# Two-block hybrid network, 256 tokens, float32 split products: LayerNorm row operations spread between halves of weights, the decay series moved to the first output products, the first head's convolution ahead of the gate scans

## What is computed

```python
for l in range(DEPTH):   # 2
    x = layer_norm(ALPHA * x + 0.5 * swiglu(x, ffn_w1[l, 0], ffn_w2[l, 0]), ln_g[l, 0], ln_b[l, 0])
    mix = hybrid_mixer(x, w_in[l], ...)
    x = layer_norm(ALPHA * x + mix, ln_g[l, 1], ln_b[l, 1])
    x = layer_norm(ALPHA * x + 0.5 * swiglu(x, ffn_w1[l, 1], ffn_w2[l, 1]), ln_g[l, 2], ln_b[l, 2])

# in the mixer's recurrence, per channel:
log_a = -LRU_C * gate_rec * jax.nn.softplus(-a_param)
a = jnp.exp(log_a)
mult = jnp.sqrt(-jnp.expm1(2.0 * log_a))

# in the last mixer, per head (8 heads):
qk = jax.nn.silu(dw_conv(jnp.concatenate([q, k], axis=-1), conv_w, conv_b))   # 3 taps along the tokens
state, hs = mlstm_chunkwise(q, k, v, i_pre, f_pre, state)                       # gates: cumulative sums and maxima
```

## Time and profile before

| | |
|---|---|
| median of 3 runs | 2186.13 us (2181.99 to 2194.47) |
| the profiled execution's own time | 2188.97 us |
| its span, first to last instruction | 2187.2 us |
| PE busy | 2145.6 us, 98% of the span |
| DVE busy | 1431.6 us, 65% |
| ACT busy | 900.1 us, 41% |
| mean granted TensorE clock | 0.994 of full speed |

### The profile page before, as it was taken

How to read it: one execution, slowest core, us unless ns; L and a number is a source line. 1 busy time by engine, 2 the same in 40 slices (tenths; PEclk the granted TensorE clock), 3 DMA queues, 4 the chain that set the end, 5 groups by cost and what they waited for, 6 DMA issues and landing times. The chain is left out here.

```text
span 2187.2 us, 35415 instructions
## 1 busy us (share of the span) xinstructions
PE 2145.6 (98%) x14986; PEld 1945.9 (89%) x14986; DVE 1431.6 (65%) x2084; ACT 900.1 (41%) x1060; POOL 18.1 (1%) x35
## 2 busy tenths in 40 slices
PE   9999999999999999999999999999999989999998
PEld 8998999999989989999899768888788878999996
DVE  5556877685566548876765677877666456666665
ACT  4333365343343334383433353222344334443442
POOL 0000000000000000000000000000000000000000
PEclk9999999999999999999999999999999999999999
DMA  9654555666566555455564432222112232232331
GB/s 346 228 181 186 193 193 200 233 259 232 183 257 235 193 193 191 179 180 203 217 240 185 159 129 77 77 77 77 65 52 78 87 116 78 97 136 78 116 116 58
DMA packets 28925, 348.94 MB, mean 160 GB/s; under 512 B 2976, under 2 KB 5408, under 8 KB 8352
## 3 DMA queue, kind: packets, MB, share of 16 engines
q1 hardware_dynamic: 24672, 313.42, 38.8%
q0 software_dynamic: 4096, 33.26, 3.8%
HBM read 345.62 MB, written 1.05 MB: 158 GB/s over the span
## 5 line engine op out<-in xcount | busy, mean ns | idle before, releaser
L2071 DVE TENSOR_TENSOR w_lo<-ring,w_hi 128x2048 fp32r<-128x2048 f32 x290 | 661.8, 2290 | 417.6 <-ACT w_hi L1497 413.0
L1497 ACT ACTIVATE w_hi<-ring 128x2048 fp32r<-128x2048 f32 x290 | 555.7, 1917 | 700.0 <-PE banks L778 472.3
L773 PE MATMUL banks<-x_hi,w_hi 128*128 128x256 f32 x2112 | 505.2, 280 | 0.2 <-ACT w_hi L1497 0.2
L774 PE MATMUL banks<-x_lo,w_hi 128*128 128x256 f32 x2112 | 504.2, 280 | 0.0
L773 PEld LDWEIGHTS banks<-x_hi,w_hi 128*128 128x128 f32 x2112 | 399.2, 189 | 1.1 <-issue 1.1
L774 PEld LDWEIGHTS banks<-x_lo,w_hi 128*128 128x128 f32 x2112 | 399.5, 189 | 0.0
L778 PE MATMUL banks<-x_hi,w_lo 128*128 128x256 f32 x2112 | 288.8, 279 | 7.9 <-DVE w_lo L2071 7.9
L778 PEld LDWEIGHTS banks<-x_hi,w_lo 128*128 128x128 f32 x2112 | 264.5, 189 | 8.7 <-DVE w_lo L2071 8.7
L1068 PE MATMUL banks<-x_hi,w_hi 128*128 128x512 f32 (+1 forms) x664 | 236.8, 370 | 1.2 <-DVE x_lo L2412 1.2
L1069 PE MATMUL banks<-x_lo,w_hi 128*128 128x512 f32 (+1 forms) x664 | 229.1, 358 | 0.0
L1531 ACT ACTIVATE arena<-banks 128x512 f32<-128x512 f32 (+5 forms) x178 | 79.7, 471 | 284.4 <-PE banks L1072 165.2
(11 more groups left out here) (367 smaller groups left out, 2808.4 us busy)
## 6 DMA issues: line engine op xcount, KB each, us to landing
ring<-weights SPq DMA_DIRECT2D x147, 2048.0 KB, 7.8
arena<-mods POOLq DMA_DIRECT2D x11, 2048.0 KB, 11.6
bcast<-lnrows POOLq DMA_DIRECT2D x12, 512.0 KB, 10.0
ring<-weights SPq DMA_DIRECT2D x2, 1024.0 KB, 9.9
xrow<-x SPq DMA_DIRECT2D x1, 1024.0 KB, 5.2
arena<-hy_consts POOLq DMA_DIRECT2D x1, 1024.0 KB, 15.4
xrow<-ctx_rows POOLq DMA_DIRECT2D x1, 1024.0 KB, 5.3
out<-xrow SPq DMA_DIRECT2D x4, 256.0 KB, 2.0
```

Source lines behind the costliest of these rows:

```text
L773: nc.tensor.matmul(out, hi[:, k, t * P:(t + 1) * P], x_h[:, k, :], start=k == 0, stop=False)
L774: nc.tensor.matmul(out, hi[:, k, t * P:(t + 1) * P], x_l[:, k, :], start=False, stop=False)
L1497: nc.scalar.activation(hi, raw, ACT.Copy).then_inc(w_hi_done, 1)
L2071: v.tensor_tensor(lo, raw, hi.bitcast(F32), ALU.subtract).then_inc(w_lo_done, 1)
```

## The change

It has three parts, and adds or removes no product and no transfer.

1. `rows_gained` becomes `row_gained(l, n, r, step)`, one operation of 128x1024 at a time. In the mixer the four stand behind the `weights_lo` calls of `yg` 3 0, 3 1, 4 0 and 4 1; in the feed-forwards behind those of j = 2 and j = 3, one per half.
2. The decay series is cut into four steps, which stand behind the first four `weights_lo` calls of the first feed-forward's output products (`down`), and ACT's Exp moves behind the first `weights_hi` there.
3. `qk_conv(0)`, the convolution of head 0, moves ahead of the gate scans, and its two tanh on ACT move ahead of the next `weights_hi`.

```diff
--- before.py
+++ after.py
@@ -1524,6 +1524,9 @@
                         mod_copy(MOD_GROUPS.index((l, "up", f)))
                 for q in range(DOWN_HALVES - 2):
                     after(l, "down", f, q // 2, q % 2)
+                    if (l, f, q) == (0, 0, 0):
+                        act.wait_ge(sp_abs, 1)
+                        nc.scalar.activation(small[:, 16:32], small[:, 0:16], ACT.Exp).then_inc(sp_exp, 1)
                     if (l, f) == (DEPTH - 1, 1):
...
             copy(cond[:].rearrange("p a b -> p (a b)"), c2[:, C2["cond"]:C2["cond"] + 16], S2["cond_done"], ACT.Silu)
-            act.wait_ge(sp_abs, 1)
-            nc.scalar.activation(small[:, 16:32], small[:, 0:16], ACT.Exp).then_inc(sp_exp, 1)
             for l in range(DEPTH):
                 half_b, half_m, decay = half_bs[:, l, :], half_ms[:, l, :], decays[:, l, :]
                 ffn(l, 0)
...
                     A.drain().then_inc(S2["gate_rows"], 1)
                     act.sem_inc(free[b], 1)
+                    ml_silu(0)
                 after(DEPTH, "qkv", i, 0)
...
                     act.wait_ge(S2["gate_ab"], 2)
                     copy(g_u[0:64, 0:SEQ], g_u[0:64, SEQ:ROWS], S2["em_in"], ACT.Exp, scale=-1.0)
-                    ml_silu(0)
                 b = filled(act, i, "ml", "z")
...
-            def rows_gained(l, n):
-
-                filled(dve, l, "layer", "turn", n, 3)
-                dve.wait_ge(row_in, 32 * (3 * l + n) + 32)
-                for r in range(RT):
-                    v.tensor_tensor(xrow[:, r, :], xrow[:, r, :], bcast[:, 0, :], ALU.mult)
-                v.drain()
-                for r in range(RT):
-                    x = v.tensor_tensor(xrow[:, r, :], xrow[:, r, :], bcast[:, 1, :], ALU.add)
-                x.then_inc(S2["rows_ok"], 1)
-                v.drain()
+            def row_gained(l, n, r, step):
+
+                if r + step == 0:
+                    filled(dve, l, "layer", "turn", n, 3)
+                    dve.wait_ge(row_in, 32 * (3 * l + n) + 32)
+                v.drain()
+                x = v.tensor_tensor(xrow[:, r, :], xrow[:, r, :], bcast[:, step, :], (ALU.mult, ALU.add)[step])
+                if r + step == 2:
+                    x.then_inc(S2["rows_ok"], 1)
+                    v.drain()
 
             def ffn(l, f):
                 for j in range(FJ):
-                    if j == 2 and l + f:
-                        rows_gained(*((l, 1) if f else (l - 1, 2)))
-                    after(l, "up", f, j, 0)
-                    after(l, "up", f, j, 1)
+                    for side in range(2):
+                        after(l, "up", f, j, side)
+                        if j in (2, 3) and l + f:
+                            row_gained(*((l, 1) if f else (l - 1, 2)), side, j - 2)
                     b = filled(dve, l, "layer", "up", f, j, 1)
                     released(dve, l, "layer", "up", f, j, 0)
...
                     after(l, "down", f, q // 2, q % 2)
+                    if l + f == 0 and q < 4:
+                        decay_series(q)
                     if q == FT // 4:
...
-            def log1p(dst, y, tmp, tmp2):
...
-                for odd in (13.0, 11.0, 9.0, 7.0, 5.0, 3.0, 1.0):
...
+            def decay_series(step):
+
+                dst, y, tmp, tmp2 = (small[:, 16 * n:16 * n + 16] for n in (3, 1, 4, 5))
+                if step == 0:
+                    v.scalar_tensor_tensor(both(0), ap, -1.0, ap, ALU.mult, ALU.min).then_inc(sp_abs, 1)
+                    v.tensor_scalar(half_bs[:], lcs[:, :, LCOL["rg_b"]:LCOL["rg_b"] + 16], 0.5, None, ALU.mult)
+                    v.tensor_scalar(half_ms[:], lcs[:, :, LCOL["b_merge"]:LCOL["b_merge"] + 16], 0.5, None, ALU.mult)
+                    v.tensor_scalar(both(2), ap, -1.0, 0.0, ALU.mult, ALU.max)
+                if step == 1:
+                    dve.wait_ge(sp_exp, 1)
+                    v.tensor_scalar(tmp, y, 2.0, None, ALU.add)
+                    v.drain()
+                    v.reciprocal(tmp, tmp)
+                    v.drain()
+                    v.tensor_tensor(tmp, tmp, y, ALU.mult)
+                    v.drain()
+                    v.tensor_tensor(tmp2, tmp, tmp, ALU.mult)
+                    v.drain()
+                    v.tensor_scalar(dst, tmp2, 2.0 / 17.0, 2.0 / 15.0, ALU.mult, ALU.add)
+                for odd in ((), (), (13.0, 11.0, 9.0, 7.0), (5.0, 3.0, 1.0))[step]:
                     v.drain()
                     v.tensor_tensor(dst, dst, tmp2, ALU.mult)
                     v.drain()
                     v.tensor_scalar(dst, dst, 2.0 / odd, None, ALU.add)
                 v.drain()
-                v.tensor_tensor(dst, dst, tmp, ALU.mult)
-                v.drain()
+                if step == 3:
+                    v.tensor_tensor(dst, dst, tmp, ALU.mult)
+                    v.drain()
+                    v.tensor_tensor(dst, dst, small[:, 32:48], ALU.add)
+                    v.drain()
+                    v.tensor_scalar(decays[:].rearrange("p l k -> p (l k)"), dst, -LRU_C / 2, None, ALU.mult)
+                    v.drain()
...
-            v.scalar_tensor_tensor(both(0), ap, -1.0, ap, ALU.mult, ALU.min).then_inc(sp_abs, 1)
...
-            dve.wait_ge(sp_exp, 1)
-            log1p(small[:, 48:64], small[:, 16:32], small[:, 64:80], small[:, 80:96])
-            v.tensor_tensor(small[:, 48:64], small[:, 48:64], small[:, 32:48], ALU.add)
-            v.drain()
-            v.tensor_scalar(decays[:].rearrange("p l k -> p (l k)"), small[:, 48:64], -LRU_C / 2, None, ALU.mult)
-            v.drain()
...
                 split(hg_hi[:], hg_lo[:], a_t[:]).then_inc(hg_done, 1)
-                rows_gained(l, 0)
                 for q in (3, 4, 5):
                     for side in range(2):
                         after(l, "yg", q, side)
+                        if q < 5:
+                            row_gained(l, 0, side, q - 3)
...
+            def qk_conv(i):
+                v.tensor_copy(ml_c[:, 0:MLC], c2[:, i * MLC + C2["ml"]:(i + 1) * MLC + C2["ml"]])
+                if i:
+                    head_gates(i)
+                v.drain()
+                released(dve, i, "ml", "q")
+                released(dve, i, "ml", "k")
+                v.tensor_scalar(q_ml[:], q_pad[:, 0:SEQ], ml_c[:, 0:1], ml_c[:, 3:4], ALU.mult, ALU.add)
+                k2 = k_ml[:].rearrange("p (w n) -> p w n", w=2)
+                v.tensor_scalar(k2, k_pad[:, :, 0:SEQ], ml_c[:, 4:5], ml_c[:, 7:8], ALU.mult, ALU.add)
+                for j in (1, 2):
+                    v.drain()
+                    v.scalar_tensor_tensor(q_ml[:], q_pad[:, j:j + SEQ], ml_c[:, j:j + 1], q_ml[:], ALU.mult, ALU.add)
+                    v.scalar_tensor_tensor(k2, k_pad[:, :, j:j + SEQ], ml_c[:, 4 + j:5 + j], k2, ALU.mult, ALU.add)
+                v.drain().then_inc(S2["qk_conv"], 1)
+                dve.sem_inc(S2["copied"], 1)
+
+            qk_conv(0)
             dve.wait_ge(S2["gate_rows"], 1)
             v.tensor_tensor_scan(g_m[0:32, :], g_t[0:32, :], g_b[0:32, :], 0.0, ALU.mult, ALU.add)
...
             for i in range(ML_HEADS):
-                v.tensor_copy(ml_c[:, 0:MLC], c2[:, i * MLC + C2["ml"]:(i + 1) * MLC + C2["ml"]])
                 if i:
-                    head_gates(i)
-                v.drain()
...
-                v.drain().then_inc(S2["qk_conv"], 1)
-                dve.sem_inc(S2["copied"], 1)
+                    qk_conv(i)
                 dve.wait_ge(S2["qk_th"], i + 1)
                 v.scalar_tensor_tensor(q_ml[:], z512[:, 0, 0:SEQ], 1.0, q_ml[:], ALU.add, ALU.mult)
                 v.scalar_tensor_tensor(k_ml[:], z512[:, 1, :], 1.0, k_ml[:], ALU.add, ALU.mult)
```

More of the change, by code:

```diff
@@ L2206, in split, with both @@
                 return v.tensor_tensor(dst_lo, src, dst_hi.bitcast(F32), ALU.subtract)
-            def log1p(dst, y, tmp, tmp2):
-                v.tensor_scalar(tmp, y, 2.0, None, ALU.add)
-                v.drain()
-                v.reciprocal(tmp, tmp)
-                v.drain()
-                v.tensor_tensor(tmp, tmp, y, ALU.mult)
-                v.drain()
-                v.tensor_tensor(tmp2, tmp, tmp, ALU.mult)
-                v.drain()
-                v.tensor_scalar(dst, tmp2, 2.0 / 17.0, 2.0 / 15.0, ALU.mult, ALU.add)
-                for odd in (13.0, 11.0, 9.0, 7.0, 5.0, 3.0, 1.0):
+            lcs = colsb[:].rearrange("p (l c) -> p l c", l=DEPTH)
+            ap = lcs[:, :, LCOL["a_param"]:LCOL["a_param"] + 8]
+            def both(n):
+                return small[:, 16 * n:16 * n + 16].rearrange("p (l k) -> p l k", l=DEPTH)
+            def decay_series(step):
[17 more added lines that the diff above has]
+                for odd in ((), (), (13.0, 11.0, 9.0, 7.0), (5.0, 3.0, 1.0))[step]:
                     v.drain()
@@ L2234, in _ @@
             dve.wait_ge(c_in, 48)
-            lcs = colsb[:].rearrange("p (l c) -> p l c", l=DEPTH)
-            ap = lcs[:, :, LCOL["a_param"]:LCOL["a_param"] + 8]
-            def both(n):
```

(11 more changed lines are left out.)

10 lines of the change are left out of this document (removed).

## The result

| | before | after |
|---|---|---|
| median of 5 runs | 2185.81 us (2181.99 to 2194.47) | 2171.13 us (2170.84 to 2174.64) |
| the profiled execution's own time | 2188.97 us | 2170.84 us |
| its span | 2187.2 us | 2169.0 us |
| PE busy | 2145.6 us | 2137.3 us |
| span less PE busy | 41.6 us | 31.7 us |

The ratio is 0.9925, with a 95% interval of 0.9907 to 0.9942: 0.7% faster. Between the two medians lie 14.7 us; the ratio, which is not that of the medians, stands for 16.4 us, and its interval begins at 12.7. PE is idle 9.9 us less. The other 8.3 us by which the two profiled spans differ are in PE's busy time, and only in part the change's doing, as the experiments show.

The account below looks back on a forecast made before the run. PE was taken to bound the kernel, busy 2145.6 us, 98% of the span. The terms 3.57 + 1.70 + 3.29 + 0 + 0 + 4.40 = 12.96 us, off the median 2186.13, gave 2173.2 us; range 2164 to 2186.

Parts of the forecast that it names:

- The mixers, 3.57 and 3.29: In the mixers of layers 0 and 1, PE's waits for `w_lo` of 3.57 and 3.29 us go whole.
- The clock behind the stall, 1.70: Layer 0's mixer: the half clock from 362.20 to 365.60 is given back, 1.70 us; nothing in layer 1.
- Feed-forward rows, 0: Twelve row operations in three feed-forwards: each delays a `w_lo` by 1.2 to 1.3 us, hidden by slack, worth 0.
- Decay series, 0: At the start, taking away 20 small DVE operations gives 0; at the new place `w_hi` is 0.3 us late, price 0.
- Head 0, 2.70 of waiting: In head 0 the 4.05 us `qk_done` wait goes and the `w_lo` wait grows by 1.35 to 2.18: 2.70 us gained.
- Head 0, 1.70 of clock: In head 0 the half clock from 1840.20 to 1843.60, behind the 4.05 us wait, is given back: 1.70 us.
- The sum: All terms over the kernel: 3.57 + 1.70 + 3.29 + 0 + 0 + 4.40 = 12.96 us, from the median 2173.2 us.
- the stall moves on to the scans: Rival, chance 0.12: the clock falls behind head 0's 2.18 us wait; head 0 gains 2.7 or loses 0.15, not 4.40.
- more than I count: Rival, chance 0.08: the 9.10 us low stretch behind L1111 is shorter by chance, another 4.55 us: 2168.6 us.

Follow-up runs that it names:

- the two parts alone: The kernel before with only the mixer rows moved, 2178.22 us, and with only head 0's convolution and tanh moved, 2183.51 us, against 2186.67 us.
- the second comparison: The changed kernel timed once more, unaltered, against the kernel before: 2170.87 us, ratio 0.9936 (0.9917 to 0.9954).

## Why the prediction was right, and where it was not

The time forecast was 2173.2 us, 2171.13 came. The waits of the mixers and of head 0 went as forecast; one term of the clock did not come, one move was worth more than the nothing it was priced at, and that the total still came so near is luck. By its steps:

- *The mixers, 3.57 and 3.29.* Both waits went, and the rows alone gave 8.5 us against 8.56 forecast. What was off is the margin: 1.37 us in layer 0 by the trace of before, 2.77 in the profile after (354.78 against 357.55), where the products had the spacing of 118 ns.
- *The clock behind the stall, 1.70.* Shown: filling the wait alone brings 1.7 us back in the trace. That layer 1 keeps its clock behind 3.29 us was the chance of one execution. Of the four profiles with the old order and empty waits all had the half clock in layer 0, and two in layer 1, where the run of the head alone waited only 2.01 us and kept it. So on the mean this term was too small, by half of the 1.4 us that the filled wait of layer 1 gave.
- *Feed-forward rows, 0.* Together with the decay series 1.0003 (0.9985 to 1.002), and no wait at j = 2 or 3 in the trace.
- *Decay series, 0: too small.* At its new place it costs nothing, as forecast. ACT was even less late than the 0.3 us I gave: the table load (1.28 us) ran while ACT waited for DVE, and the next `w_hi` then still waited for PE:

```profile
146.59 1.28 ACT L1529 ACT_TABLE_LOAD   x1
149.02 0.22 ACT L1529 ACTIVATE small<-small 128x16 f32<-128x16 f32 x1 [1.14 <-DVE small L2220]
150.21 1.92 ACT L1497 ACTIVATE w_hi<-ring 128x2048 fp32r<-128x2048 f32 x1 [0.98 <-PE banks L919]
```

  But "gives 0" at its old place was read from a profile in which PE was late itself. The first row is of the profile of before, the others of the run of the head alone, which has the series at the start too:

```profile
14.06:17.47 3.41, 3.41 (x18) 3.41 (x17) 3.41 (x2) 1.33 (x1) 0.00 (x0) 0.50 1.09 455
```

```profile
30.95 0.27 DVE L2250 TENSOR_SCALAR decays<-small 128x16 f32<-128x16 f32 x1
31.29 4.49 DVE L2071 TENSOR_TENSOR w_lo<-ring,w_hi 128x2048 fp32r<-128x2048 f32 x2
```

```profile
33.64 0.62 PE L778 MATMUL banks<-x_hi,w_lo 128*128 128x256 f32 x3 [2.11 <-DVE w_lo L2071]
```

  Of the five profiles with the series at the start, three have a half clock at 13 to 14 us and no wait here; the two without it have a wait, 2.11 and 1.85 us, for the `w_lo` that stands behind the series. None of the nine profiles with the series moved has it. By these traces the move saves some 2 us in executions in which nothing else has made PE late, and nothing in the others. The comparison of that run (3.3 us less to 4.4 more) can't show it.
- *Head 0, 2.70 of waiting.* The `qk_done` wait went, and the wait at L1072 became 2.07 us for the 2.18 forecast. Across head 0 PE's instructions gained 2.9 us in the trace, of the 4.40 forecast for it.
- *Head 0, 1.70 of clock: the step that failed.* "Behind the 4.05 us the clock was half for 1840.20 to 1843.60: 1.70 again" counted this as returned. But the sum had itself made a wait of 2.18 us some 9 us ahead of it, and the half clock moved behind that one, in all four profiles with an empty wait of 2.07 us there and in none of the nine with some 0.8 us. At other places a wait of 2.0 to 2.5 us had a half clock behind it in some profiles and none in others. I had this as the rival in which the stall moves on to the scans, at 0.12; in head 0 it was the right one.
- *The sum.* The waits gave 9.9 us instead of 9.6, the clock 1.7 instead of 3.4 and perhaps 0.7 in layer 1. That is about 12 us, the start adds some 2 us in part of the executions, and the two parts alone gave 11.7. The first comparison exceeds the 12 us by 2 to 3; its interval begins at 12.7 us, and the second comparison, with 14.0 us by its ratio, at 10.1. The spans of the two profiles differ by 18.1 us. Counted from their instructions, 9.9 of these are PE's idle time, 3.3 the clock (half of its half-clock time on work; 1.7 of it is the stretch at 14 us) and 3.9 the spacing, of which the last section tells; 1.1 are left. Whether the change makes the longer spacing rarer, or these executions drew it so, stays open. The forecast was near the result because the clock term was too large while the start and the spacing, which it did not count, made up for it: luck.

The rival "more than I count" did not come: the half clock at L1111 was 10.2 us long in both profiles of the changed kernel, as in that of before (9.10 us of it behind the end of the wait). The Trainium skill (TensorE: Matmul & The Clock Gate, Part 1) says of a kernel's start that the count of products at the low clock is run-variable. The trace agrees for the start, and the same is seen in layer 1, but not in head 0, where every profile with the wait of 2.07 us had it.

## What to carry to other kernels

Read which operation of the late engine stands ahead of the one that is waited for, and count how long after its start the other engine wants it; that margin sizes the whole change. When a change shortens one wait and lengthens another, price the clock at the new wait too, as the wait of 2.07 us cost 1.5 us more behind it, and before counting a half clock as a gain, look whether the operands behind it would be there any sooner. Before pricing a move at nothing because the late engine shows no wait there, look whether a half clock ahead had made that engine late. Where single executions spread by 3 to 5 us, judge terms of 1 or 2 us by the same instruction in two traces, not by medians.

## What was not expected of the hardware

TensorE ran the same 128x256 products at one of two spacings, 113.3 or 117.8 ns from start to start, at a granted clock of 1.00 (the first in layer 1, the second in layer 0 of the rows above). A spacing holds for tens to hundreds of us, and in the places that were looked at it changes only where a stage or a wait ends or products of another shape come between; where it is which differs between executions of one kernel. Counted from the instructions, without those at half clock, 5,500 of some 9,600 such steps have the longer spacing in the profile of before, and 4,800 in that of after. That is 3 us; all 9,600 at the longer spacing would be 43 us. Products of 512 columns have two spacings as well, 229 and 233 ns.

Idle time, clock and spacing together account for the spans. When the span of each of the 14 profiles is taken less PE's idle time, half of the half-clock time on work, 4.5 ns for each step at the longer spacing (5,100 to 8,100 of both sorts) and the products of no use, 2103.2 to 2106.9 us are left, all but one within 2103.2 to 2105.0, while the spans reach from 2161.6 to 2191.9. The two runs with the filled wait at L1111 differ by 8.3 us in span: the slower one has 9.2 us more by the spacing and 3.3 us less of idle time. The Trainium skill (TensorE: Matmul & The Clock Gate, Wait — 56ns, not 53.3ns?) gives the columns divided by the clock and some 2.5 ns more, an estimate of 109 ns for 256 columns; neither spacing of the trace agrees with it. What chooses between the two was not found, and no run here was made to settle it.
